# Three attentions of paired heads: the logits of the next tile issued ahead of this tile's turning and output

## The reference

```
# dsa: 16 heads, keys and values made from a latent of 128, only the 128 best keys of a query count
p = softmax(logits * dh ** -0.5 + bias, over selected keys);  o = p @ values
# nsa: 8 heads in 4 pairs, three branches weighted by gates
o = gate0 * attend(compressed blocks) + gate1 * attend(selected keys) + gate2 * attend(window)
# fox: 8 heads in 4 pairs
logits = q @ k.T * scale + c[query] - c[key];  p = softmax(logits, causal);  o = p @ v
```

## Time and profile before

| what | value |
|---|---|
| median of 3 runs | 3154.63 us (3153.62 to 3155.69) |
| the profiled execution, its own time | 3152.18 us |
| its span, from the first to the last instruction | 3150.4 us |
| outside the span | 1.8 us |
| mean granted TensorE clock | 0.959 |
| dsa attention, from the first logits to the last output | about 1279 to 1380 us of the span |
| nsa attention | about 2478 to 2575 us |
| fox attention | about 2576 to 2623 us |

### The profile page before, as it was taken

How to read it: one execution, slowest core, us unless ns; L and a number is a source line. 1 busy time by engine, 2 the same in 40 slices (tenths; PEclk the granted TensorE clock), 3 DMA queues, 4 the chain that set the end, 5 groups by cost and what they waited for, 6 DMA issues and landing times.

```text
span 3150.4 us, 47831 instructions
## 1 busy us (share of the span) xinstructions
PE 2866.1 (91%) x19030; PEld 2082.4 (66%) x19030; DVE 1427.0 (45%) x2257; ACT 1033.0 (33%) x1526; POOL 230.3 (7%) x220
## 2 busy tenths in 40 slices
PE   4998889888999989888999969999989897899998
PEld 1566666645888744465888848888555555688875
DVE  6466555625333227555333243333134665533335
ACT  1323322204442122544442144431111464344214
POOL 1122222201000010311000000000000100000000
PEclk9999999988999989999999989999869998999999
DMA  4222323332322211012223212232121001232212
GB/s 190 92 92 92 118 102 105 96 107 69 105 93 105 82 45 60 21 41 80 93 93 118 82 37 97 93 113 95 49 74 56 32 2 33 88 104 95 105 58 97
DMA packets 45842, 260.79 MB, mean 83 GB/s; under 512 B 4952, under 2 KB 7400, under 8 KB 26888
## 3 DMA queue, kind: packets, MB, share of 16 engines
q1 hardware_dynamic: 45128, 254.20, 23.1%
q10 hardware_dynamic: 576, 4.57, 0.4%
HBM read 256.59 MB, written 2.15 MB: 82 GB/s over the span
## 4 chain that ended last, share of the span: by engine, by line
PE 83%; DVE 7%; ACT 3%; issue 3%; DMA 2%; POOL 1%; PEld 1%; DVEq 0%; SPq 0%; POOLq 0%; ACTq 0%; PEldq 0%
PE psum L192 81%; PE psum L1571 1%; DMA weights<-in_ada 1%; PEld psum L192 1%; DVE weights L228 1%; DVE ln_rstd L1135 0%; DVE attention_in L1650 0%; ACT nsa_probs L1607 0%; POOL join L508 0%; POOL join L497 0%; POOL XT_pairs L501 0%; DVE rms_rstd L1215 0%; DVE dsa_probs L1680 0%; DVE group_norm L766 0%; DVE ff_weights_lo L1247 0%
## 5 line engine op out<-in xcount | busy, mean ns | idle before, releaser
L1247 DVE TENSOR_TENSOR ff_weights_lo<-weights,ff_weights_hi 128x1024 fp32r<-128x1024 f32 (+1 forms) x120 | 159.7, 1332 | 330.2 <-ACT ff_weights_hi L1244 330.2
L1247 DVE TENSOR_TENSOR ffn_weights_lo<-weights,ffn_weights_hi 128x1024 fp32r<-128x1024 f32 (+1 forms) x120 | 159.7, 1332 | 321.9 <-ACT ffn_weights_hi L1244 321.9
L192 PE MATMUL psum<-ff_in_hi,ff_weights_hi 128*128 128x512 f32 x704 | 276.3, 392 | 21.0 <-DVE ff_in_lo L1144 17.6
L192 PE MATMUL psum<-ffn_in_hi,ffn_weights_hi 128*128 128x512 f32 x704 | 275.9, 392 | 17.6 <-DVE ffn_in_lo L1223 14.2
L1244 ACT ACTIVATE ffn_weights_hi<-weights 128x1024 fp32r<-128x1024 f32 (+1 forms) x120 | 137.4, 1147 | 447.7 <-PE psum L192 447.7
L1244 ACT ACTIVATE ff_weights_hi<-weights 128x1024 fp32r<-128x1024 f32 (+1 forms) x120 | 137.4, 1147 | 445.7 <-PE psum L192 445.7
L192 PE MATMUL psum<-ff_in_lo,ff_weights_hi 128*128 128x512 f32 x704 | 275.8, 392 | 0.0
L192 PE MATMUL psum<-ff_in_hi,ff_weights_lo 128*128 128x512 f32 x704 | 275.5, 391 | 0.0
L192 PE MATMUL psum<-ffn_in_lo,ffn_weights_hi 128*128 128x512 f32 x704 | 275.1, 391 | 0.0
L192 PE MATMUL psum<-ffn_in_hi,ffn_weights_lo 128*128 128x512 f32 x704 | 275.1, 391 | 0.0
L192 PEld LDWEIGHTS psum<-ff_in_hi,ff_weights_hi 128*128 128x128 f32 x704 | 133.4, 189 | 51.0 <-issue 19.2
(11 more groups left out here) (459 smaller groups left out, 5155.7 us busy)
## 6 DMA issues: line engine op xcount, KB each, us to landing
weights<-in_ada SPq DMA_DIRECT2D x96, 512.0 KB, 4.4
weights<-in_ff_in SPq DMA_DIRECT2D x44, 1024.0 KB, 4.8
weights<-in_ffn_in SPq DMA_DIRECT2D x44, 1024.0 KB, 4.8
weights<-in_ff_out SPq DMA_DIRECT2D x16, 1408.0 KB, 5.8
weights<-in_ffn_out SPq DMA_DIRECT2D x16, 1408.0 KB, 5.9
weights<-in_rwkv SPq DMA_DIRECT2D x8, 1792.0 KB, 8.2
weights<-in_fox_qkv SPq DMA_DIRECT2D x4, 1536.0 KB, 6.6
residual<-in_x ACTq DMA_DIRECT2D x2, 2048.0 KB, 9.7
```

The lines of the kernel that those rows point to most:

```text
L192: return nc.tensor.matmul(out, lhsT, rhs, start=start, stop=stop)
L1247: return nc.vector.tensor_tensor(sp_.lo[u][:, 0:width], slot[s][:, u * width:(u + 1) * width], sp_.hi[u][:, 0:width].bitcast(F32), ALU.sub ...
```

## The change

TensorE's loop begins one turn earlier and issues L of unit t + 1 where it issued L of unit t. VectorE's loop begins one turn earlier too; the block of S is moved to the front of a turn, and behind it comes M of unit t + 1 (the old block with n for t), then V and the low part of an output. ScalarE is not touched.

```diff
             def pe(pe):
...
-                for t in range(N + 3):
-                    if t < N:
-                        u = units[t]
-                        if t >= 2:
-                            pe.wait_ge(masked, 2 * (n0 + t) - 2)
-                        if made is not None and first[t]:
+                for t in range(-1, N + 3):
+                    if t + 1 < N:
+                        n = t + 1
+                        u = units[n]
+                        if n >= 2:
+                            pe.wait_ge(masked, 2 * (n0 + n) - 2)
+                        if made is not None and first[n]:
                             pe.wait_ge(made.keys_copied, u["pair"] + 1)
...
-                            ins = mm(ps[:, 2 * (t % 2) + hh, 0:u["w"]], u["query"][hh], u["keys"][hh], True, "extra" not in u)
+                            ins = mm(ps[:, 2 * (n % 2) + hh, 0:u["w"]], u["query"][hh], u["keys"][hh], True, "extra" not in u)
...
                         ins.then_inc(logits, 1)
                     if t in made_at:
...
             def dve(dve):
...
-                for t in range(N + 5):
-                    if t < N:
-                        u = units[t]
...
-                    if t in made_at:
-                        made.dve(dve, made_at[t], TR)
-                    if parts and t >= 4 and t - 4 < N and last[t - 4]:
...
+                for t in range(-1, N + 5):
                     if 1 <= t < N + 1:
                         n = t - 1
                         w = units[n]["w"]
...
+                    if t + 1 < N:
+                        n = t + 1
+                        u = units[n]
+                        w = u["w"]
+                        dve.wait_ge(logits, n0 + n + 1)
+                        if n >= 2:
+                            dve.wait_ge(exped, 2 * (n0 + n) - 2)
...
+                    if t in made_at:
+                        made.dve(dve, made_at[t], TR)
+                    if parts and t >= 4 and t - 4 < N and last[t - 4]:
+                        i = units[t - 4]["pair"]
+                        dve.wait_ge(out_hi, p0 + i + 1)
+                        nc.vector.tensor_tensor(out[1][:, i, :], ps[:, O + i % 2, :], out[0][:, i, :].bitcast(F32),
+                                                ALU.subtract).then_inc(out_lo, 1)
```

More of the change, by code:

```diff
@@ L1543, in pe @@
                                 for hh in range(2):
-                                    ins = mm(ps[:, 2 * (t % 2) + hh, q * NB:(q + 1) * NB], u["query"][hh][:, q * P:(q + 1) * P], u["keys"][hh])
+                                    ins = mm(ps[:, 2 * (n % 2) + hh, q * NB:(q + 1) * NB], u["query"][hh][:, q * P:(q + 1) * P], u["keys"][hh])
                         for hh in range(0 if "blocks" in u else 2):
-                            ins = mm(ps[:, 2 * (t % 2) + hh, 0:u["w"]], u["query"][hh], u["keys"][hh], True, "extra" not in u)
+                            ins = mm(ps[:, 2 * (n % 2) + hh, 0:u["w"]], u["query"][hh], u["keys"][hh], True, "extra" not in u)
                         if "extra" in u:
                             for hh in range(2):
-                                ins = mm(ps[:, 2 * (t % 2) + hh, 0:u["w"]], *u["extra"][hh], False, True)
+                                ins = mm(ps[:, 2 * (n % 2) + hh, 0:u["w"]], *u["extra"][hh], False, True)
                         ins.then_inc(logits, 1)
@@ L1681, in dve @@
                                                     ALU.mult, ALU.bypass if gate is None else ALU.mult).then_inc(scaled, 1)
+                    if t + 1 < N:
[5 more added lines that the diff above has]
+                            dve.wait_ge(exped, 2 * (n0 + n) - 2)
+                        if "blocks" in u:
+                            by_tile = sx[:, n % 2, 0, 0:w].rearrange("p (q h n) -> p q h n", q=QT, h=2)
+                            by_head = sx[:, n % 2, 0, 0:w].rearrange("p (e n) -> p e n", n=NB)
+                            least, done = small.least, small.so_far()
+                            nc.vector.tensor_tensor(by_tile, ps[:, 2 * (n % 2):2 * (n % 2) + 2, 0:QT * NB].rearrange("p h (q n) -> p q h n", n=NB),
+                                                    u["mask"].rearrange("p (q h n) -> p q h n", q=QT, h=2), ALU.add).then_inc(small.sem, 1)
+                            dve.wait_ge(small.sem, done + 1)
+                            nc.vector.tensor_reduce(least, by_head, AX.X, ALU.min).then_inc(small.sem, 1)
+                            dve.wait_ge(small.sem, done + 2)
+                            nc.vector.tensor_tensor(by_head, by_head, least.unsqueeze(2).to_broadcast([P, 2 * QT, NB]),
+                                                    ALU.subtract).then_inc(masked, 2)
+                        for hh in range(0 if "blocks" in u else 2):
+                            if masks_made is not None:
+                                dve.wait_ge(masks_made, 2 * n + hh + 1)
+                            nc.vector.tensor_tensor_reduce(
+                                out=sx[:, n % 2, hh, 0:w], in0=ps[:, 2 * (n % 2) + hh, 0:w], in1=u["mask"][hh], scale=1.0, scalar=3e38,
+                                op0=ALU.add, op1=ALU.min, accum_out=stat[:, n % 4, LEAST, hh:hh + 1]).then_inc(masked, 1)
```

## The result

The changed kernel takes **3133.03 us** (median of 4 runs, 3130.09 to 3136.09) against 3154.12 for the kernel before in the same session. The ratio is 0.9936, with a 95% interval of 0.9924 to 0.9948: 21 us less, where 20.4 were foretold. The execution profiled is the longest of the four, 3136.09 us (span 3134.3).

The account below looks back on a forecast made before the run. TensorE, busy 91% of the span, was taken as the bound, with 34.4 us idle in the three attentions. Gains of 11.5 (dsa), 6.3 (nsa) and 2.6 (fox) sum to 20.4, giving 3134.2 us; range 3127 to 3146.

Parts of the forecast that it names:

- dsa, 11.5 foretold: dsa stage: 1.60 us a pair over six pairs, 9.6, plus 1.9 at its start and end.
- The made hole: dsa, TensorE idle between the made keys and values and T(128): shrinks from 1.15 to 0.79 us, 0.36 gained.
- T(512)'s hole: dsa, TensorE idle while T(512) waits for late S(512): the hole of 1.24 us a pair goes.
- K is no longer last: dsa, behind the made pair: keys are made 0.97 us before values and E(512) starts earlier, so V ends the hole.
- Behind the scaling is a renumbering and gives nothing: VectorE's order: M and S alternate as before, so putting M behind S costs or gives nothing.
- nsa, 6.3 foretold: nsa stage: 1.5 us a pair over three periods, 4.5, plus 1.5 at the start and 0.3 at the end.
- The clock, 1 us either way: nsa: the granted clock's rise to 2.4 GHz coming two microseconds sooner or later shifts the time 1 us either way.
- fox, 2.6 foretold: fox stage: waits of 4.9 us less 2.3 that stay at start, end and in small ones.
- L's moved wait: TensorE: L moved earlier waits for M(t-1), which precedes S(t-2) on VectorE, so it never ends last; zero cost.
- C did not keep its waits (first rival): ScalarE in nsa and fox: E just ahead of C keeps the steady holes, 6.8 us lost, 3141; chance 0.13.
- V did not become late (second): VectorE in dsa: V late behind S(256) and M(384), 6.7 us lost, 3141, or 16.8 lost, 3151; chance 0.10.
- The chain T, C, E, S did not set the pace (third): nsa: the earlier L delays T and that chain, lengthening each tile; 14 us slower, 3169; chance 0.05.

Follow-up runs that it names:

- made pair first: Changed kernel, but in the seven pair-making turns TensorE issues the made pair ahead of L(384) and VectorE does V ahead of M(384); 3126.12 us, ratio 0.9916.
- matmuls alone: TensorE's new order with VectorE's old loop, against the kernel before; 3130.25 us, ratio 0.9929.
- filler: Changed kernel plus two unused matmuls in nsa, repeating the second unit's L ahead of the third unit's L; 3135.67 us, ratio 0.9941.
- four copies: Changed kernel plus four chained 128x512 SBUF copies on VectorE ahead of V in the seven pair-making turns; 3154.66 us, ratio 1.0004.
- one copy: Changed kernel plus one 128x512 SBUF copy on VectorE ahead of V in the seven pair-making turns; 3131.35 us, ratio 0.9938.
- changed kernel again: The unaltered changed kernel, timed again beside the kernel before on the same chip; 3134.04 us, ratio 0.9937.
- dsa alone: New orders of TensorE and VectorE in dsa only, old ones in nsa and fox, against the kernel before; 3145.48 us, ratio 0.9972.

## Why the prediction was right

**dsa, 11.5 foretold, 11.4 measured.** The pair was to fall by 1.60 and fell by 12.98 - 11.39 = 1.59; six of them make 9.5, which leaves the 1.9 foretold for start and end. The made hole came out at 0.88 where 0.79 was worked out, since T(128) began 0.15 us behind the end of V and not 0.06; so it gave 0.27 and not 0.36. T(512)'s hole gave its 1.24. The other 0.08 is recorded busy time (10.59 to 10.51), for which the prediction had no term, so that 1.59 meets 1.60 this closely is luck. "K is no longer last" holds (no wait on K is left), and M(384) ran where it was put.

One reason in that step was too narrow. M(384) *beside the making of the pair* was given as what takes the second hole away. The run with the made pair first has M(384) behind V, with TensorE already past the making, and that hole stays away too. What matters is that L(384) is ahead of T(128) and O(384), not that it is ahead of the made pair; putting it there left V's hole unfilled, 5 us that this order gives away.

**"Behind the scaling is a renumbering and gives nothing."** Right for the steady turns, shown by the run with the matmuls alone, and 1.1 us off at the start of dsa, where V's place counts.

**nsa, 6.3 foretold, 7.5 measured: the mis-sized term.** From the first L to the first T(512), before 17.97 us and after 16.85, the start gave 1.1 and not 1.5: the hole in front of the first T was filled, as foretold, but M(512), which has to wait for S(384), passed on only 0.85 of it to the second T(384) (15.48 to 14.63). Three periods of the pair, 22.51 - 20.73 = 1.78 each, gave 5.3 and not 4.5. From the last pair's T(512) to fox's first L, the end gave 1.1 and not 0.3, and why was not followed up. The pair's idle time fell by 1.56, as worked out (1.5); the other 0.22 is recorded busy time (20.67 to 20.45). In dsa's pair it is the 0.08. I put it down to the matmuls on either side of a hole, whose recorded times overlap when no hole lies between; that is argued, not tried. "The clock, 1 us either way" was no term at all: the filler moved the rise and the stage stayed.

**fox, 2.6 foretold, 3.3 measured.** Of the 2.3 us that were to stay, 1.5 did: 0.5 at the start for 0.7, 1.0 at the end for 1.4, and no small ones.

**L's moved wait costs zero.** Right in the steady turns; the 0.5 in fox at its start is the one new place where it ends last.

**The rivals.** C did not keep its waits (first rival). V did not become late (second): VectorE was 0.89 us ahead where 1.0 had been worked out, and the four copies show what would have come otherwise, though at more than the rival's price, since the clock fell too. S(256) lengthened by 0.58 as its row had let expect (0.64). The chain T, C, E, S did not set the pace (third): nsa's pair has 0.28 us idle.

**The sum.** 20.4 foretold, 22.3 in the stages, about 21 and 19 in the two comparisons of whole times. The 2 us too little, in nsa and fox, were inside the range.

## What to carry to other kernels

In a pipeline whose engine queues are written out by hand, look for a matmul whose inputs have long been there behind one that must wait, and for each hole that is left, ask which independent work could stand in it: here the same L, one place further back, filled the last one. A hole is worth filling only where TensorE sets the pace behind it; ahead of a wait for another engine, as at the start of nsa, little comes back. When the whole time scatters by more than the effect, compare the lengths of stages.

## What the hardware showed that was not expected

**A hole costs more than its length where the granted clock falls, and of equal holes only some are followed by a fall.** With four copies ahead of V, TensorE's first hole in dsa was 3.47 us, and the T(512) two rows later took 1.93, where in the changed kernel, behind a hole of 1.09, it took 1.06 (timeline of TensorE, then the stage's window):

```profile
1290.93 0.63 PE L1572 MATMUL psum<-const_all,dsa_probs 128*128 128x128 f32 x4 [3.47 <-DVE dsa_values L1976]
...
1292.29 1.93 PE L1572 MATMUL psum<-const_all,dsa_probs 128*128 128x128 f32 x8
```

```profile
1281.28:1388.74 107.46, 89.21 (x688) 58.19 (x686) 85.51 (x267) 66.86 (x176) 37.78 (x56) 0.94 0.01 4
```

The stage's clock is 0.94, 1.00 in the changed kernel, and the same 688 matmuls are busy 89.21 us for 83.17, 6.0 more: with the 10.9 us of holes that makes the 16.9. The added holes cost over half as much again as they are long; the changed kernel's, of 0.88 and once 1.09, left the clock at 1.00, and behind the one of 1.68 in the run with one copy T(512) took its 1.06 as well.

The fall does not come behind every hole. Six more of 2.28 or 2.29 follow the first. Behind the one at 1330.55, shown with the experiment, O(384) took 0.88, as in the changed kernel; behind the one ahead of it it took 1.55:

```profile
1316.27 0.66 PE L1572 MATMUL psum<-const_all,dsa_probs 128*128 128x128 f32 x2 [2.28 <-DVE dsa_values L1976]
1316.87 1.55 PE L192 MATMUL psum<-attention_in,dsa_values 128*64 128x128 f32 x12
```

The first, third, fifth and seventh hole are followed by such slow matmuls, the others are not. What makes the difference between holes of the same length stays open.

**Part of the scatter arises in stretches that nothing touched, and goes with their clock.** In the profile after, dsa begins 4.8 us later than before. Of that, 3.7 arise in the recurrence (first matmuls at 176 and 654 us of the profile before), whose instructions the change doesn't touch. Its stretch from 490 to 570 us, before and then after:

```profile
490.00:570.00 80.00, 73.99 (x1250) 51.48 (x1250) 45.84 (x73) 25.07 (x36) 17.19 (x13) 0.98 0.28 92
```

```profile
490.00:570.00 80.00, 74.58 (x1198) 53.42 (x1198) 43.22 (x69) 22.20 (x32) 16.96 (x13) 0.91 0.26 91
```

At a clock of 0.91 for 0.98 fewer matmuls fall into the same 80 us. It is not the new order that lowers it: the profiles of the changed kernel again and of dsa alone show 0.91 there as well, those of the matmuls alone and of the made pair first, which have the new order too, 0.98. The mean clock of a whole execution goes with its time only loosely: 0.956 and 3136.09 us, 0.960 and 3130.09, both the changed kernel, but also 3131.25 and 3135.39 with 0.959 each. What decides which clock a run gets there stays open. The run with the filler, whose three stages are those of the changed kernel, took from 3127.10 to 3136.59 us.

**Beside GpSimd some of VectorE's operations take longer and others do not.** Of the four equal copies shown above, the two that ran beside a mask addition took 0.69 and 0.83, the two behind it 0.43; the addition's row:

```profile
1327.01 1.58 POOL L2003 TENSOR_TENSOR dsa_mask<-index_scores,bias_near 128x256 f32<-128x256 f32 x2 [1.12 <-DVE dsa_stat L1675]
```

M, which reads PSUM, was not lengthened: of the M(384) shown with the result the first head took 0.56, the second, from 1331.52, 0.55, although an addition ran beside it from 1331.68. S(384) at the start of nsa, with its 2.26, runs beside a memset of GpSimd (2481.40 to 2483.20 in the changed kernel); the next S(384), with GpSimd idle, takes 0.87. Whether the start of nsa would be shorter with that memset elsewhere was not tried. The Trainium skill, SBUF — State Buffer, "SBUF: two separate sides", says that GpSimd shares one port pair with those VectorE operations that run in a two-port mode or have two inputs in SBUF, and that the pair is held for a whole instruction. The copies and M agree that some operations share and others do not; GpSimd's rows are too rough to tell whether the wait was for a whole instruction.
